# Value pages of the cache loaded from ScalarE's queue, keys alone on SyncE's

## The reference

```python
q, k, v, u = _project(x, pos, norm1_w, w_in, q_norm_w, k_norm_w)   # RMSNorm, h @ w_in, q/k norm, rope, GLU
attn = differential attention   # softmax of component 0 minus lam * softmax of component 1, 4 heads
conv = _conv_mixer(u_ext, ...)  # causal depthwise conv of 31 taps, LayerNorm, swish
x = x + concat([attn, conv]) @ w_out
x = x + _moe(RMSNorm(x), ...)   # 32 experts, top 4, clamped SwiGLU
```

```python
k_past = cache_k[l][page_table].reshape(bs, n_past, DIFF_HEADS, 2, QK_DIM)
v_past = cache_v[l][page_table].reshape(bs, n_past, DIFF_HEADS, V_DIM)
```

## Time and profile before

| | |
|---|---|
| median of 3 runs | 1743.2 us (1741.07 to 1750.26) |
| the profiled execution | 1743.68 us |
| its span | 1742.0 us |
| PE busy | 1464.7 us (84%) |
| DVE busy | 781.1 us (45%) |
| ACT busy | 356.1 us (20%) |
| q1 (SyncE's loads) | 560.20 MB, 81.5% of 16 engines' span |
| q10 (ScalarE's) | 20.00 MB, 3.2% |

### The profile page before, as it was taken

The page is one execution under the profiler, slowest core; times in us unless marked ns, Lnnn a source line. Parts: engine busy times, 40 slices in busy tenths (PEclk is TensorE's granted clock), DMA queues, the critical chain, the costliest instruction groups (busy, mean ns, idle before and its releaser), DMA issues.

```text
span 1742.0 us, 32083 instructions
## 1 busy us (share of the span) xinstructions
PE 1464.7 (84%) x11950; PEld 589.3 (34%) x11951; DVE 781.1 (45%) x1158; ACT 356.1 (20%) x822; POOL 95.4 (5%) x173
## 2 busy tenths in 40 slices
PE   3868886768898868999999898999998998998870
PEld 2433332335433343333333332332333332332220
DVE  2789877997886335211323222232232131131316
ACT  3212202232320221111211211211212122121220
POOL 0000002000000000000000000000000000000000
PEclk8989996688998857999999999999999999999995
DMA  9558798878989765579999999999999999999976
GB/s 326 190 176 270 268 356 289 262 258 282 332 295 308 253 257 216 234 312 404 428 418 415 427 399 397 426 404 395 418 423 402 410 428 394 402 428 428 427 324 251
DMA packets 127181, 598.10 MB, mean 343 GB/s; under 512 B 20392, under 2 KB 20406, under 8 KB 101915
## 3 DMA queue, kind: packets, MB, share of 16 engines
q1 hardware_dynamic: 109088, 560.20, 81.5%
q10 hardware_dynamic: 8522, 20.00, 3.2%
q0 software_dynamic: 9504, 17.06, 2.6%
HBM read 589.36 MB, written 25.87 MB: 353 GB/s over the span
## 4 chain that ended last, share of the span: by engine, by line
PE 39%; DMA 20%; DVE 2%; issue 1%; ACT 0%; DVEq 0%; SPq 0%; ACTq 0%
PE bank L1509 23%; DMA wts<-in_w_gate_up 14%; PE bank L1546 8%; DMA wts<-in_w_down 6%; PE bank L1528 4%; DVE v_ring L2135 1%; PE bank L1499 1%; PE bank L1616 1%; PE bank L1557 1%; PE bank L1597 0%; DVE q_b L2135 0%; DMA h_tok<-h_rows,v_tok 0%; ACT k_T L1153 0%; DVEq L2123 0%; ACT k_T L1136 0%
## 5 line engine op out<-in xcount | busy, mean ns | idle before, releaser
L1509 PE MATMUL bank<-wts,h_T 128*32 128x512 f32 x4032 | 444.0, 596 | 17.9 <-DMA wts<-in_w_gate_up 17.9
L2057 DVE TENSOR_SCALAR q_T<-bank 128x512 f32<-128x512 f32 x32 | 22.1, 692 | 636.2 <-PE bank L1509 636.2
L1546 PE MATMUL bank<-wts,k_T 128*32 128x512 f32 x2048 | 229.7, 599 | 9.6 <-issue 4.9
L1509 PEld LDWEIGHTS bank<-wts,h_T 128*32 128x32 f32 x4032 | 129.3, 111 | 317.9 <-issue 288.3
L1656 DVE TENSOR_TENSOR wts<-wts,q_b 128x1024 f32<-128x1024 f32 x128 | 157.6, 1231 | 23.6 <-DMA wts<-in_cache_k 17.3
L1528 PE MATMUL bank<-wts,h_T 128*32 128x512 f32 x992 | 129.1, 662 | 45.6 <-DMA wts<-in_w_gate_up 43.8
L1659 DVE TENSOR_REDUCE sc<-wts 128x16 f32<-128x1024 f32 x128 | 156.2, 1220 | 4.4
L1143 ACT ACTIVATE h_T<-bank 128x512 f32<-128x512 f32 x66 | 35.9, 595 | 571.5 <-PE bank L1499 571.5
L1546 PEld LDWEIGHTS bank<-wts,k_T 128*32 128x32 f32 x2048 | 65.3, 111 | 151.7 <-issue 138.8
L1221 PE MATMUL bank<-wts,h_T 128*8 128x128 f32 (+1 forms) x480 | 91.9, 449 | 13.1 <-DMA wts<-in_w_in 7.1
L1153 ACT ACTIVATE k_T<-bank 32x256 f32<-32x256 f32 x256 | 95.8, 374 | 14.6 <-PE bank L1546 11.2
(11 more groups left out here) (328 smaller groups left out, 1361.1 us busy)
## 6 DMA issues: line engine op xcount, KB each, us to landing
wts<-in_w_gate_up SPq DMA_DIRECT2D x126, 2048.0 KB, 15.4
wts<-in_w_down SPq DMA_DIRECT2D x64, 2048.0 KB, 18.2
wts<-in_cache_k SPq DMA_DIRECT2D x256, 256.0 KB, 3.6
v_ring<-in_cache_v SPq DMA_DIRECT2D x160, 256.0 KB, 3.9
wts<-in_cache_v SPq DMA_DIRECT2D x96, 256.0 KB, 3.8
wts<-in_w_in SPq DMA_DIRECT2D x5, 2048.0 KB, 24.1
wts<-y_rows SPq DMA_DIRECT2D x4, 2048.0 KB, 15.0
wts<-in_w_out ACTq DMA_DIRECT2D x1, 4096.0 KB, 19.9
```

Source lines behind the costliest of these rows:

```text
L1509: m = nc.tensor.matmul(PS[part][p0:p0 + 32, :], lhs[:, 32 * b:32 * b + 32], rhs[:, part * F + half * 512:part * F + half * 512 + 512], sta ...
L1546: m = nc.tensor.matmul(PS[4][p0:p0 + 32, :], act_T[0][:, k, a0:a0 + 32], chunk[c][:, k, n * 512:(n + 1) * 512], start=(c == 0 and k == 0), ...
```

## The change

The helper load_group now takes the engine and its registers. SyncE keeps the key loads; load_values moves to ScalarE, into its own order of the schedule:

- the first four value groups go out at the head of P 1 on ScalarE, ahead of its normalisation;
- groups 4 to 35 are loaded one value step later in the order than before (the groups of step n - 1 instead of n);
- groups 40 and on keep their step, at its head, ahead of the exponents and of copy_u;
- groups 36 to 39 go out in stage 7 of P 4, ahead of w_out.

In the schedule three entries at P 2 give no value step any more, so value step 0 stands after key step 19 instead of 16, and each later value step stands where the third one before it stood.

```diff
         for s in range(1, TILES + 1):
             if s > 1:
-                plan(("P", s), 1, both=True)
-            plan(("P", s - 1), 1 if s > 1 else 0, both=s > 1)
-            plan(("P", s), 1 if s > 1 else 3, both=s > 1)
+                plan(("P", s), 1, both=s > 2)
+            plan(("P", s - 1), 1 if s > 1 else 0, both=s > 2)
+            plan(("P", s), 1 if s > 1 else 3, both=s > 2)
...
+        def load_group(eng, page_regs, dst, done, cache, n):
+
+            eng.load(page_regs, pages_sb[0:1, n * GP:(n + 1) * GP])
+            for p in range(GP):
+                page = eng.snap(page_regs[p], min_val=0, max_val=cache.shape[0] - 1)
+                eng.dma_start(dst[:, p, :], cache[bass.ds(page, 1)].rearrange("a p n -> (a p) n")).then_inc(done, 16)
...
             def load_keys(n):
                 after(sp, kred_done, n + 1 - RING)
-                load_group(k_ring[:, n % RING], k_full[n % RING], kc, n)
-
-            def load_values(m):
-                if m == V_TAIL - VRING:
-                    sp.wait_ge(kred_done, NB * NG)
-                    for r in range(RING):
-                        load_group(k_ring[:, r], k_full[r], vc, V_TAIL + r)
-                if m < V_TAIL:
-                    after(sp, pv_done, v_before(m) + 1)
-                    load_group(v_of(m), v_loaded(m)[0], vc, m)
+                load_group(sp, page_regs, k_ring[:, n % RING], k_full[n % RING], kc, n)
...
             def value_step(b, g):
-                n = value_no[0]
-                value_no[0] += 1
-                for m in groups_of(n // NG, n % NG):
-                    if m < V_FEW:
-                        load_values(m + RING)
-                for m in groups_of((n - 2) // NG, (n - 2) % NG) if n > 1 else ():
-                    if V_FEW <= m < NB * NG - VRING:
-                        load_values(m + VRING)
...
-            def part_p(s):
-                yield
-                if s == 1:
-                    for m in range(RING):
-                        load_values(m)
-                yield from [None] * 4
-                if s == TILES:
-                    sp.wait_ge(*filled(a_full, a_no[("P", TILES)][0]))
-                    for m in range(V_FEW + RING, V_FEW + VRING):
-                        load_values(m)
...
@@ -831,6 +800,10 @@
+                if s == 1:
+                    act.wait_ge(pages_in, 16)
+                    for m in range(RING):
+                        load_values(m)
                 act.wait_ge(x_loaded, 16 * (s + 1))
...
                         if s == TILES:
+                            for m in range(V_FEW + RING, V_FEW + VRING):
+                                load_values(m)
                             act.dma_start(w_out_sb, w_out[0].rearrange("(k p) n -> p k n", p=P)).then_inc(wout_in, 16)
...
@@ -1079,7 +1054,28 @@
+            def load_values(m):
+                if m == V_TAIL - VRING:
+                    act.wait_ge(kred_done, NB * NG)
+                    for r in range(RING):
+                        load_group(act, page_regs, k_ring[:, r], k_full[r], vc, V_TAIL + r)
+                if m < V_TAIL:
+                    after(act, pv_done, v_before(m) + 1)
+                    load_group(act, page_regs, v_of(m), v_loaded(m)[0], vc, m)
...
             def value_step(b, g):
+                n = value_no[0]
+                value_no[0] += 1
+                for m in groups_of((n - 1) // NG, (n - 1) % NG) if n else ():
+                    if m < V_FEW:
+                        load_values(m + RING)
+                for m in groups_of((n - 2) // NG, (n - 2) % NG) if n > 1 else ():
+                    if V_FEW <= m < NB * NG - VRING:
+                        load_values(m + VRING)
                 if b < NB and g == 6:
                     act.wait_ge(sub_done, b + 1)
```

More of the change, by code:

```diff
@@ L498, in _ @@
             page_regs = [sp.alloc_register(f"page{p}") for p in range(GP)]
-            def load_group(dst, done, cache, n):
-                sp.load(page_regs, pages_sb[0:1, n * GP:(n + 1) * GP])
-                for p in range(GP):
-                    page = sp.snap(page_regs[p], min_val=0, max_val=cache.shape[0] - 1)
-                    sp.dma_start(dst[:, p, :], cache[bass.ds(page, 1)].rearrange("a p n -> (a p) n")).then_inc(done, 16)
             def load_keys(n):
                 after(sp, kred_done, n + 1 - RING)
-                load_group(k_ring[:, n % RING], k_full[n % RING], kc, n)
-            def load_values(m):
-                if m == V_TAIL - VRING:
-                    sp.wait_ge(kred_done, NB * NG)
-                    for r in range(RING):
-                        load_group(k_ring[:, r], k_full[r], vc, V_TAIL + r)
-                if m < V_TAIL:
-                    after(sp, pv_done, v_before(m) + 1)
-                    load_group(v_of(m), v_loaded(m)[0], vc, m)
+                load_group(sp, page_regs, k_ring[:, n % RING], k_full[n % RING], kc, n)
             def load_q(b):
@@ L529, in key_step @@
                     load_q(b + 2)
-            value_no = [0]
             def value_step(b, g):
-                n = value_no[0]
-                value_no[0] += 1
-                for m in groups_of(n // NG, n % NG):
-                    if m < V_FEW:
-                        load_values(m + RING)
-                for m in groups_of((n - 2) // NG, (n - 2) % NG) if n > 1 else ():
-                    if V_FEW <= m < NB * NG - VRING:
-                        load_values(m + VRING)
                 if g == 9 or b == 0 and g == 2:
@@ L551, in _ @@
             load_q(1)
-            def part_p(s):
-                yield
-                if s == 1:
-                    for m in range(RING):
-                        load_values(m)
-                yield from [None] * 4
-                if s == TILES:
-                    sp.wait_ge(*filled(a_full, a_no[("P", TILES)][0]))
-                    for m in range(V_FEW + RING, V_FEW + VRING):
-                        load_values(m)
-            run_with_samples(key_step, value_step, {part: part_p(part[1]) if part[0] == "P" else iter(())
-                                                    for part in a_no})
+            run_with_samples(key_step, value_step, {part: iter(()) for part in a_no})
             def load_chunk(c, e, chunk=gu_chunk):
@@ L1080, in key_step @@
                 pass
-            def value_step(b, g):
+            page_regs = [act.alloc_register(f"value_page{p}") for p in range(GP)]
+            def load_values(m):
[6 more added lines that the diff above has]
+                    load_group(act, page_regs, v_of(m), v_loaded(m)[0], vc, m)
+            value_no = [0]
+            def value_step(b, g):
+                n = value_no[0]
[6 more added lines that the diff above has]
+                        load_values(m + VRING)
                 if b < NB and g == 6:
```

## The result

The changed kernel takes 1794.4 us (median; 1790.9 to 1796.2) against 1743.1 us: a ratio of 1.028, 95% interval 1.0261 to 1.0299, so 51 us slower. The forecast was 1762 and its range ended at 1782, at most 1784. The profiled execution has a span of 1789.2 us, 47.2 more than before. The direction was right, the size was not.

The account below looks back on a forecast made before the run. Before 603 us the fullest engine was taken to bind: VectorE from 56 to 397 us, TensorE from 397 to 470 and 547 to 603. Terms 6.2 - 3 - 15 + 17 + 3 + 10 = +18 gave 1762 us, own range 1753 to 1782.

Parts of the forecast that it names:

- (a): Start: four value groups on ScalarE ahead of P 1's normalisation delay the first key step; +6.2 us, bounds 3 to 8.
- (b): First value steps three key steps later: TensorE's wait for pmax and VectorE's after it mostly covered; -3 us, 0 to -5.
- (c): P 3 and P 4: with keys alone on SyncE, VectorE's waits mostly shrink; -15 us, bounds 0 to -25.
- (d): Q part: value pairs on ScalarE stand between a copy and the next exponents; +17 us, bounds 5 and 46.
- (e): 397 to 547 us: pairs ahead of copy_u delay TensorE, partly offset by fewer value-page waits; +3 us, -3 to 8.
- (f): End, 547 to 603 us: six groups issued on ScalarE delay exponents and copy_u for TensorE; +10 us, 3 to 15.
- The DMA engines bind P 3 and P 4: Rival: full DMA engines there mean a key queue without values gains nothing; +33, 1777 us; chance 0.12.
- ScalarE's gaps hide the issues: Rival: in Q and at the end idle ScalarE absorbs the issues; -11, 1733 us; chance 0.16.
- Gains and costs cancel: Rival: P 3 and P 4 win 20, Q costs 10, the end 5; +1, 1745 us; chance 0.17.
- Values late throughout: Rival: ScalarE issues values so late that TensorE waits for pages throughout; about 1820 us; chance 0.05.
- square waits under 3 us each: Sign of being right: VectorE's waits for ScalarE's square of q and k in P 3 and P 4 stay that short.
- square waits that persist: Sign of being wrong: 5 us waits for ScalarE's square remain, meaning they never came from late values.

Follow-up runs that it names:

- start_sync: The changed kernel with the first four value groups issued by SyncE behind q_b's rows, all others still on ScalarE; 1.0196 of the kernel before.
- p_part: The changed kernel with ScalarE issuing value groups 0 to 39 alone and SyncE the rest; 1.0061 of the kernel before, 1753.7 us.
- c_only: The changed kernel with ScalarE issuing value groups 4 to 39 alone, SyncE the rest; value steps at new places; 1.0016 of the kernel before.
- sched_only: The kernel before with only the new places of the value steps, all loads still on SyncE; 0.9973 of the kernel before.
- pool_late: pool_all with GpSimd's first four groups waiting for the sample's rows and the tap products back at the end of P 4; 0.9952, 1734.7 us.
- pool_old: pool_late with the value steps at their old places; 0.9929 of the kernel before, 1731 us.
- act_only: The changed kernel with the value steps at their old places, so only the loads move to ScalarE; 1.0296 of the kernel before.
- more_sync: The changed kernel with value groups 36 to 39 on SyncE, all others on ScalarE; 1.0197 of the kernel before.
- wout_pool: The changed kernel with the load of w_out issued on GpSimd's queue at the same point instead of ScalarE's; 1.0261 of the kernel before.
- q_on: The changed kernel with SyncE issuing value groups 0 to 39, ScalarE 40 to 123 and the key ring's four; 1.0165, 1771.9 us.
- loads_last: The changed kernel with a value step's loads on ScalarE moved behind its exponents and copy_u; 1.0218 of the kernel before.
- half_act: start_sync with value groups 4 to 35 loaded with half of their columns, same number of issues; 1.0200 of the kernel before.
- half_sync: sched_only with value groups 4 to 35 loaded with half of their columns, every load on SyncE; 0.9963 of the kernel before.
- pool_all: The changed kernel with all value groups but the last four on GpSimd, those on SyncE, tap products in Q 0; 0.9989 of the kernel before.
- pool_wout: pool_old with w_out issued on ScalarE behind u_T of P 4; 0.9943 of the kernel before.

## Why the prediction was wrong

Term by term, the prediction's number, then the measured one at R 4 or at the end of the stretch:

- **(a)**, +6.2: 11.7 (after less start_sync) and 11.1 (p_part less c_only). The mechanism was right, the size at R 4 not. The four groups took 6.66 us and the normalisation stood 7.46 us for them, 1.87 us a group instead of the 1.55 of the earlier trace rows. At P 1 the two pairs of kernels differ by 8.1 and 5.2 us, which agrees with 7.46 within the spread; the bounds were 3 to 8. The remaining 3.6 and 5.9 us appear later, in the first pair up to P 4, in the second mostly after Q 16; their cause stays open.
- **(b)**, -3: -4.2 (sched_only). The number lies within the bounds by luck. The two waits it was built on, 12.04 for pmax and 5.39 for the square, are 11.90 and 5.83 with the new places. Of the gain 0.3 us is there at P 4; the rest came behind it, 2.6 between R 3 and R 4, where the text put 0.
- **(c)**, -15: +6.0 (c_only less sched_only). This is the step that failed, by 21 of the 32 us between forecast and result. It said "ScalarE's new issues lie mostly beside projections of TensorE here", and priced them at nothing. They stand in front of the copies of h_T, for which the next projection waits, and behind w_out they hold u_tok; the waits for keys and late values turned into these. From P 1 to P 4 c_only takes 166.4 us and sched_only 167.2, where -15 was forecast; of the 6.0, 1.9 are there at P 1, before the two differ in order, 2.9 at Q 2 and 6.4 at Q 16, so where the rest arose is not shown. A second thing that (c) had wrong is its sum: it took the square's 5.39 us of P 2 as gone by (b), and most of the rest as caused by SyncE's queue. With the issues on an engine outside the loop the gain is smaller than 15 where the value steps stand as in this kernel: pool_late is 7.2 us ahead of sched_only at P 4, before VectorE is held. With the steps at their old places pool_old is 10.6 us ahead of before at P 4 and 13.4 at Q 2. On ScalarE with the old places (act_only) 6 us were won up to P 4, and 12 lost behind w_out. What the text took from the earlier trace rows, that "value groups stand behind w_out in the same queue", was seen and not priced; it costs 6.5 us at the eviction of u_tok and about 7 at Q 2 (more_sync). The reason given was wrong too, since it is the bytes in flight and not the common queue (wout_pool).
- **(d)**, +17: 14.0 at Q 16 between sched_only and q_on, 15.9 counted from Q 2's 1.9 us lead. Right, with 12 pairs issued in q_on between the first and the last unit's exponents, where the text counted 15; and so is the sign by which it was to be seen, 11.9 us of waits for exponents in Q after.
- **(e)**, +3: from Q 16 to R 3 q_on takes 198.7 us, sched_only 190.5: +8.2. Under-priced, at the bound of 8. The text counted the pair ahead of copy_u at two places; loads_last, which moves the pair behind the copy and the exponents, has 3.6 us back by R 3. That more places are the reason is argued, not shown.
- **(f)**, +10: R 3 to R 4 takes 51.3 us in q_on and 40.2 in sched_only, +11.1. Right.

The sum at R 4, -4.2 + 11.4 + 6.0 + 14.0 + 8.2 + 11.1 = 46.5, stands against 45.3 us there; the span has 2 us more, and the medians of the runs 4 more still. (c) made 21 us of the miss, (a) and (e) about 5 each, (d) 3 the other way.

**The rivals.** *The DMA engines bind P 3 and P 4* had (c) at 0 and 1777 us, nearer in number, but its mechanism falls by half_act and half_sync, which have 1.6 and 4.2 us for half of the value bytes. *ScalarE's gaps hide the issues*: falls, for (d) and (f) came in full; a pair took 2.38 us of issues alone in most places, its page numbers come on top, and 2.4 us was the point at which this rival decided. In Q they hid most of the issues all the same: 12 pairs at 3.1 us are 37 us, and 14 to 16 were paid. *Gains and costs cancel*: falls with (c). *Values late throughout*: falls; TensorE's waits for pages shrank up to P 4, and one of 9.9 us stands behind w_out. The rule of the Trainium skill weighed there (DMA: Bandwidth & Descriptors, Issuing engines are not separate DMA queues), that another issuing engine only saves its sequencer's time, usually small: by that rule, little of the 13.4 us of pool_old would be there; the trace disagrees, since that time is 3.1 us per megabyte on a queue that was late.

Of the signs: first key step near 62, it came at 64.3; no key waits, 1.3 us in sum; square waits under 3 us each, wrong (5.9, 8.4 and 8.7); a Q part over 114 us, right (130.5). The prediction said what square waits that persist would mean, that they never came from late values. That holds for half of them: with values in time and no issues on ScalarE (pool_old), 10.7 of the 20.9 us of the earlier trace rows remain. What sets these isn't shown.

## What to carry to other kernels

When a transfer's issue moves to another engine, price it where that engine stands in its own order: each issue delays the next copy or exponent for which the bound engine waits. ScalarE was idle for 75% of the Q part, and still 14 to 16 of some 37 us of issues were paid there. Look for an engine that nobody waits for, here GpSimd: the same loads but the last four groups, with the steps at their old places, won 12 us there and lost 52 on ScalarE (act_only). Before two kernels are compared stage by stage, look for single instructions that are far longer than their like: three of the four GpSimd kernels had one of 6 to 7 us, as large as the differences between them. And a number that comes out right, as (b)'s did, needs its waits looked up before it counts as understood.

## What the runs showed of the hardware that was not expected

**A VectorE instruction held by GpSimd.** In pool_all the tap products of GpSimd stand in Q. GpSimd, then VectorE:

```profile
282.21 7.53 POOL L703 TENSOR_TENSOR wts<-ot,w_T 128x1024 f32<-128x1024 f32 x4
```

```profile
282.76 7.00 DVE L1674 TENSOR_TENSOR stq<-stq,nlam 128x1 f32<-128x1 f32 x1
```

A product of one number per partition, 0.16 us in sched_only (284.21), took 7.00 us, to the end of all four GpSimd products, and Q 2 came late by as much. With the products at the end of P 4 it occurs too, by chance of timing: in pool_late the 8x8 product at 267.22 took 7.15 us, to the end of GpSimd's products that began at 266.81, and in pool_wout the key product at 260.77 took 6.39. In pool_old, before and after no VectorE instruction beside the same products took more than 2.3 us. The Trainium skill (SBUF — State Buffer, SBUF: two separate sides) says that a VectorE operation with two SBUF inputs and a GpSimd operation that reads SBUF share an exclusive lock; by that rule, the trace agrees for pool_all and pool_wout, with the addition that here GpSimd instructions in a row, four in pool_all, kept it.

**An issue is not a constant.** Four value groups took 5.58, 5.91, 6.66, 10.94 and 14.16 us of ScalarE, the last two while w_out's 4 MB were moved. On GpSimd a group's two loads took 1.13 us, also beside w_out.
